# Two-layer trunk on one core: the order of two ScalarE copies, and a separate signal for the choice of experts

## What is computed

```python
x = layer_norm(ALPHA * x + h, ln1_g[i], ln1_b[i])
s  = sigmoid(x @ router_w)                  # 256 tokens x 64 experts
sb = s + router_bias                        # top 4 of 8 groups, then the top 8 experts of those
sel   = take_along_axis(s, eidx)
gates = sel / sum(sel) * 2.5
routed[tok] += gate * ((silu(x w1[e]) * (x w3[e])) w2[e])
shared = (silu(x sw1) * (x sw3)) sw2        # one expert that all tokens use
```

## Time and profile before

| what | value |
|---|---|
| median of three runs | 1353.06 us (1351.78 to 1354.09) |
| span of the profiled execution, first to last instruction | 1355.0 us |
| PE busy | 1308.7 us, 97% |
| DVE, ACT, POOL busy | 475.9, 310.8, 80.9 us |
| the 16 DMA engines | 83.1% of the span in the hardware queue; 462 MB |

### The profile page before, as it was taken

One profiled execution on the slowest core, in us unless ns is written; L12 is line 12 of the kernel. 1 busy time (PEld: TensorE's weight loads), 2 busy tenths in 40 slices (PEclk: granted clock), 3 DMA queues, 4 the chain that ended last, 5 costly groups with the idle time before them and its releaser, 6 DMA issues.

```text
span 1355.0 us, 23118 instructions
## 1 busy us (share of the span) xinstructions
PE 1308.7 (97%) x9746; PEld 751.7 (55%) x9746; DVE 475.9 (35%) x795; ACT 310.8 (23%) x746; POOL 80.9 (6%) x93
## 2 busy tenths in 40 slices
PE   9999999999999999998999999999999998999998
PEld 4555665555555455554498467655555554554543
DVE  1584533233332223324501146232333322233244
ACT  1244422121212211121210224222222221112112
POOL 2443100000000000000100021000000000000000
PEclk9999999999999999999999999999999999999999
DMA  9820679999999999999754427899999999999991
GB/s 305 303 96 32 252 304 415 421 421 420 421 420 421 421 422 420 420 421 383 245 188 163 189 82 275 308 418 421 421 421 421 420 421 421 421 421 421 420 360 69
DMA packets 83007, 462.01 MB, mean 341 GB/s; under 512 B 7008, under 2 KB 7232, under 8 KB 34528
## 3 DMA queue, kind: packets, MB, share of 16 engines
q1 hardware_dynamic: 80896, 454.16, 83.1%
q0 software_dynamic: 2016, 6.43, 1.6%
HBM read 459.52 MB, written 1.05 MB: 340 GB/s over the span
## 4 chain that ended last, share of the span: by engine, by line
PE 75%; DMA 19%; DVE 3%; issue 1%; ACT 1%; SPq 0%; DVEq 0%
PE ps L1227 26%; DMA ring<-in_exp_w_dram 19%; PE ps L1267 12%; PE ps L884 4%; PE ps L1413 4%; PE ps L1289 4%; PE ps L1166 4%; PE ps L1063 3%; PE ps L988 3%; PE ps L1135 2%; PE ps L1087 2%; PE ps L1237 1%; PE ps L1048 1%; PE ps L1127 1%; PE ps L904 1%
## 5 line engine op out<-in xcount | busy, mean ns | idle before, releaser
L1267 PE MATMUL ps<-ring,qkT 128*32 128x512 f32 x1984 | 232.9, 595 | 4.4 <-issue 3.1
L2120 DVE TENSOR_TENSOR o_tok<-ps,o_tok 128x1024 f32<-128x1024 f32 x124 | 150.7, 1223 | 157.4 <-PE ps L1289 157.4
L2125 DVE TENSOR_TENSOR y_lo<-ps,y_hi 128x1024 fp32r<-128x1024 f32 x62 | 75.9, 1225 | 214.1 <-ACT y_hi L1645 214.1
L1227 PE MATMUL ps<-ring,xT 128*64 128x256 f32 x1008 | 124.5, 385 | 14.7 <-DMA ring<-in_exp_w_dram 14.7
L1267 PEld LDWEIGHTS ps<-ring,qkT 128*32 128x32 f32 x1984 | 61.5, 109 | 129.3 <-issue 127.5
L1227 PE MATMUL ps<-ring,pT 128*64 128x256 f32 x992 | 124.3, 385 | 6.4 <-DMA ring<-in_exp_w_dram 6.4
L1620 ACT ACTIVATE roped<-ps 128x256 f32<-128x256 f32 x64 | 24.6, 385 | 455.7 <-PE ps L1227 455.7
L1227 PE MATMUL ps<-ring,proj 128*64 128x256 f32 x1008 | 121.8, 379 | 0.2 <-DMA ring<-in_exp_w_dram 0.2
L1227 PE MATMUL ps<-ring,gb_row 128*64 128x256 f32 x992 | 121.5, 379 | 0.0
L2109 DVE SCALAR_TENSOR_TENSOR roped<-roped,rows,ps 128x256 f32<-128x256 f32 x64 | 30.7, 480 | 236.9 <-ACT roped L1620 236.9
L1227 PEld LDWEIGHTS ps<-ring,xT 128*64 128x64 f32 x1008 | 71.0, 136 | 73.5 <-issue 36.1
(11 more groups left out here) (301 smaller groups left out, 1477.8 us busy)
## 6 DMA issues: line engine op xcount, KB each, us to landing
ring<-in_exp_w_dram SPq DMA_DIRECT2D x158, 2048.0 KB, 23.1
ring<-in_exp_w_dram SPq DMA_DIRECT2D x54, 1024.0 KB, 9.0
ring<-in_od_w_in_dram SPq DMA_DIRECT2D x6, 2048.0 KB, 8.8
ring<-in_ple_w_gate_dram SPq DMA_DIRECT2D x4, 2048.0 KB, 16.1
ring<-in_ev_w_in_dram SPq DMA_DIRECT2D x3, 2048.0 KB, 20.2
ring<-in_ev_w_o_dram SPq DMA_DIRECT2D x2, 2048.0 KB, 9.9
x_tok<-in_exp_w_dram SPq DMA_DIRECT2D x4, 1024.0 KB, 8.8
ring<-in_exp_w_dram SPq DMA_DIRECT2D x8, 512.0 KB, 16.5
```

Source lines behind the costliest of these rows:

```text
L1227: ins = pe.matmul(ps[b * SLOTS:(b + 1) * SLOTS, 2, w * FE:(w + 1) * FE], xe(odd, c)[:, u * P + b * SLOTS:u * P + (b + 1) * SLOTS], views[b ...
L1267: ins = pe.matmul(ps[q:q + TILE_SLOTS, 4 + half, :], hT[:, f, h0:h0 + TILE_SLOTS], down_rows(b, f, half), start=(f == 0), stop=(f == 1))
L2120: dve.tensor_tensor(ys, ps[:, bank:bank + 2, :], ys, ALU.add).then_inc(sem("y_added"), 1)
L2125: dve.tensor_tensor(y_lo[:, :], ps[:, 4:6, :].rearrange("p b n -> p (b n)"), y_hi[:, :], ALU.subtract)\
```

## The change

ACT copies a tile's transposes ahead of writing its rounded half, for both tiles and in both layers. In `choose`, the instruction that writes `chosen` now counts up a semaphore of its own, and PE waits for that one ahead of the place matmuls, where it waited for the finished gates.

```diff
 # ACT, both layers
                 rsqrt_guess()
+                copy_T("xT_act", tp, 0)
                 x_high(0)
-                copy_T("xT_act", tp, 0)
                 router_exp(0)
                 y_begin(0)
                 rsqrt_guess()
+                copy_T("xT_act", tp, 1)
                 x_high(1)
-                copy_T("xT_act", tp, 1)
                 router_exp(1)
 # DVE, choose
-                seq(dve.tensor_scalar(own, sb_, TAKEN, None, ALU.is_equal))
+                dve.tensor_scalar(own, sb_, TAKEN, None, ALU.is_equal).then_inc(sem("chosen"), 1)
+                dve.wait_ge(sem("chosen"), NT * L + t + 1)
                 seq(dve.tensor_tensor(g1, s, own, ALU.mult))
 # PE, ahead of the place matmuls
-                pe.wait_ge(sem("router_dve"), NT * (L + 1))
+                pe.wait_ge(sem("chosen"), NT * (L + 1))
```

The rest of the diff renames semaphores. Six that PE counts up once each in the compressed branch of layer 0 (`cmp_tp`, `cmp_h`, `cmp_kv`, `cmp_rep`, `cmp_sc`, `cmp_pT`, in that order) become one, `cmp_pe`, with the waits at 1 to 6; three that ACT counts up in layer 1 (`fox_abs`, `fox_e`, `fox_ln`) become `fox_act` with the waits at 1 to 3. One pair of lines of each:

```diff
-                    dve.wait_ge(sem("cmp_kv"), 1)
+                    dve.wait_ge(sem("cmp_pe"), 3)
-                    dve.wait_ge(sem("fox_ln"), 1)
+                    dve.wait_ge(sem("fox_act"), 3)
```

More of the change, by code:

```diff
@@ L641, in _ @@
                 if src == QA:
-                    pool.wait_ge(sem("cmp_h"), 1)
+                    pool.wait_ge(sem("cmp_pe"), 2)
                 for t in range(1 if src == QA else NT):
@@ L776, in attention @@
                             ins = pe.transpose(ps[:, 6, tt * P:(tt + 1) * P], cmp_s[:, tt, :], ident)
-                        ins.then_inc(sem("cmp_pT"), 1)
+                        ins.then_inc(sem("cmp_pe"), 1)
                     if 3 <= u < U + 3:
@@ L860, in compressed_scores @@
                                         small[:, 448:448 + 2 * CMP_PAD], start=True, stop=True)
-                ins.then_inc(sem("cmp_sc"), 1)
+                ins.then_inc(sem("cmp_pe"), 1)
             def transpose_queries(t):
@@ L946, in compressed_inputs @@
                         pe.transpose(ps[:, 5, 0:CMP_LEN], qkT[0:CMP_LEN, 16, 0:P], ident[0:CMP_LEN, 0:CMP_LEN])\
-                            .then_inc(sem("cmp_tp"), 1)
+                            .then_inc(sem("cmp_pe"), 1)
                     def compressed_hidden(part):
@@ L958, in compressed_hidden @@
                         if part == 3:
-                            ins.then_inc(sem("cmp_h"), 1)
+                            ins.then_inc(sem("cmp_pe"), 1)
                     def compressed_kv():
@@ L967, in compressed_kv @@
                                             small[0:HD, half * HD:(half + 1) * HD], start=True, stop=True)
-                        ins.then_inc(sem("cmp_kv"), 1)
+                        ins.then_inc(sem("cmp_pe"), 1)
                     def compressed_spread():
@@ L974, in compressed_spread @@
                         pe.matmul(ps[:, 4, 0:HD], const[0:CMP_PAD, C_REP:C_REP + P], small[0:CMP_PAD, 384:448],
-                                  start=True, stop=True).then_inc(sem("cmp_rep"), 1)
+                                  start=True, stop=True).then_inc(sem("cmp_pe"), 1)
                     def project_tile(j, t, between=()):
@@ L1459, in attention @@
                     if L == 0 and u == 4:
-                        act.wait_ge(sem("cmp_pT"), 1)
+                        act.wait_ge(sem("cmp_pe"), 6)
                         act.activation(small_pT, ps[:, 6, 0:SEQ], ACT.Copy).then_inc(sem("cmp_pT_copied"), 1)
@@ L1540, in _ @@
                     duplicate("roped", 3, 28)
-                    act.wait_ge(sem("cmp_h"), 1)
+                    act.wait_ge(sem("cmp_pe"), 2)
                     act.activation(small[0:HD, 160:160 + N_CMP], ps[0:HD, 4, 0:N_CMP], ACT.Exp, scale=-1.0)
@@ L1553, in _ @@
                     act.wait_ge(sem("fox_z"), 1)
[L1554 to L1558, removed]
+                    act.activation(fox_t, fox_zb, ACT.Abs).then_inc(sem("fox_act"), 1)
+                    act.wait_ge(sem("fox_act"), 1)
+                    act.activation(fox_t, fox_t, ACT.Exp, scale=-1.0).then_inc(sem("fox_act"), 1)
+                    act.wait_ge(sem("fox_act"), 2)
+                    act.activation(fox_t, fox_t, ACT.Ln, bias=1.0).then_inc(sem("fox_act"), 1)
                     for j in range(4):
@@ L1775, in compressed_max @@
             def compressed_max():
-                dve.wait_ge(sem("cmp_sc"), 1)
+                dve.wait_ge(sem("cmp_pe"), 5)
                 for t in range(NT):
@@ L1942, in compressed_blocks @@
                     def compressed_blocks():
-                        dve.wait_ge(sem("cmp_tp"), 1)
+                        dve.wait_ge(sem("cmp_pe"), 1)
                         seq(dve.tensor_copy(kvT, ps[:, 4, 0:SEQ]))
@@ L1987, in _ @@
                     topk_round(8)
-                    dve.wait_ge(sem("cmp_rep"), 1)
+                    dve.wait_ge(sem("cmp_pe"), 4)
                     dve.tensor_copy(small[0:HD, 448:448 + CMP_PAD], ps[0:HD, 5, 0:CMP_PAD])
@@ L2015, in _ @@
                        .then_inc(sem("fox_z"), 1)
-                    dve.wait_ge(sem("fox_abs"), 1)
+                    dve.wait_ge(sem("fox_act"), 1)
                     seq(dve.tensor_scalar(z, z, 0.0, None, ALU.min))
-                    dve.wait_ge(sem("fox_ln"), 1)
+                    dve.wait_ge(sem("fox_act"), 3)
                     dve.tensor_tensor(logf.rearrange("p t n -> p (t n)"), z, fox_t, ALU.subtract).then_inc(sem("logf"), 1)
```

## The result

The kernel takes **1357.11 us** (median of 8 runs, 1355.74 to 1359.55) against 1353.33 us for the kernel before (8 runs, 1351.78 to 1354.53). The ratio is 1.0028, with an interval of 1.0019 to 1.0037: **3.8 us slower, 2.6 to 5.0**.

The account below looks back on a forecast made before the run. PE was taken to bound the stage from first norm to experts, the weight stream the expert loop's end. A 1.8 us later gather in each of two layers gives 3.6 us: 1353.06 + 3.6 = 1356.7 us, range 1353.2 to 1358.4.

Parts of the forecast that it names:

- The copies: ACT's copies of tile 0 run first: second copy ends at 148.23 instead of 148.39, router gains at most 0.16 us.
- ACT's chain: Tile 0 on ACT: x_high and table load fall behind the copies; exponential starts at 151.56 instead of 150.54, 1.02 us late.
- The disputed price: ACT's table load: 1.28 us by the rows, about 2.66 us by the skill page, which would make the sum about 4.4 us.
- x_lo and the hold: Tile 0: POOL's x_lo, 150.32 to 153.21, holds the choice's first TENSOR_SCALAR on DVE until 153.26, 2.16 us late.
- the bounds: Delay of tile 0's first TENSOR_SCALAR: 1.02 us if POOL doesn't hold it, 2.16 us if it does; the upper was taken.
- the other bound: Rival: POOL doesn't hold the choice up; PE loses under 0.1 us a layer, 1353.2 us. Chance 0.13.
- PE: PE's transposes of tile 1 move from 162.05 to 163.28, 1.23 us; PE stands still for 1.4 us ahead of them.
- Tile 1 and the gather: Tile 1's TENSOR_SCALAR ends 2.76 us late, DVE has 0.58 us to spare; the gather starts 1.8 us late.
- The signal: `chosen`'s own signal to PE: worth nothing by itself; in the new order saves about 0.6 us at the gather.
- The rest of the layer: Everything after the stage, DMA-bound expert loop included, moves by PE's delay, since the weight stream starts afresh in each layer.
- The rival that the weight stream takes the stall up: PE loses 1.8 us in the stage and as much less later in the layer, up to 1353.1 us. Chance 0.07.
- The sum: 1.8 us a layer, two layers: 3.6 us, added to the median of 1353.06 us.

Follow-up runs that it names:

- e3: The changed kernel, with PE waiting for the finished gates again and the choice's scores kept in PSUM: 1353.55 us, ratio 0.9993 to the kernel before.
- e4: The kernel before, old ACT order and semaphores, with POOL computing x_lo twice over: 1360.06 us, ratio 1.0042 to the kernel before.
- e2: The changed kernel with ACT's old order, keeping the choice's own signal and the renamed semaphores: 1353.80 us, ratio 0.9996 to the kernel before.
- e1: The changed kernel with PE's place matmuls waiting for the finished gates again, copies still first: 1358.96 us, ratio 1.0035 to the kernel before.
- e7: The changed kernel with POOL's x_lo subtraction cut into four instructions of a quarter each: 1353.34 us, ratio 1.0003 to the kernel before.

## Why the prediction was right

Taken against the start of the tile-0 transposes (146.57 before, 146.69 after), step by step:

- **The copies.** Forecast to end at +1.66 us, against +1.82 before; they end at 147.93 + 0.49 = 148.42, which is +1.73. The router gains 0.1 us where at most 0.16 was forecast, and loses it at the next gap, as foreseen.
- **ACT's chain.** The exponential starts at +4.99, as forecast (151.56 - 146.57 = 4.99; now 151.68 - 146.69). The disputed price is settled by the rows: the table load takes 1.28 us and ends at 151.66, and the exponential starts 0.02 us later. The 2.66 us that the Trainium skill gives for a switch (ScalarE: Activation LUTs, What ACT_TABLE_LOAD costs) do not show here. The prediction's estimate by that page was loose by a little: with 1.38 us more the exponential would have started at 151.56 + 1.38 = 152.94, ahead of x_lo's end at 153.21, and only the TENSOR_SCALAR, due 0.36 us behind the exponential's start, would have come after it.
- **x_lo and the hold.** x_lo from +3.75 to +6.64 was forecast, +3.75 to +6.62 came; the TENSOR_SCALAR was forecast to end 0.05 us behind it and did. The choice between the bounds (1.02 us if not held, 2.16 us if held) was the one that decided: it ended 2.14 us late, and e3 and e4 show the hold to be the cause. The price that the prediction gave the other bound, under 0.1 us a layer, is about what e3 measures, 0.11 and 0.09. The rule of the Trainium skill (SBUF — State Buffer, Who interferes with whom), by which such an instruction waits for the whole of POOL's, holds for 64 columns too: 1.33 us instead of 0.195.
- **PE.** Transposes of tile 1 at +16.71 forecast, +16.69 measured; the gap was forecast as 1.4 us. From the start of the last shared-expert block it is 163.38 - 160.19 = 3.19 us to the transposes, against 162.05 - 160.17 = 1.88 in the same timeline of before, so 1.31 us; the profile's own 1.14 us is shorter, since the ends of matmuls are modelled.
- **Tile 1 and the gather.** The TENSOR_SCALAR ends 170.15 - 146.69 = 23.46 us in (23.50 forecast), the gather is at 29.74 (29.83 forecast). 1.70 and 1.65 us a layer instead of 1.8: `sel` is late by 2.06 us (175.52 - 146.69 against 173.34 - 146.57) where the TENSOR_SCALAR is late by 2.72, so DVE had 0.66 us to spare, not the 0.58 us of its idle row. PE had another 0.36: the gather started 0.51 us after `sel` was done before (174.10 to 174.61) and starts 0.15 us after it now (176.28 to 176.43).
- **The signal.** Forecast worth nothing alone, and 0.6 us a layer at the gather in the new order. It measured 0.0 (e2), and 0.73 and 0.75 (e1 against after): sized too small by some 0.1 us.
- **The rest of the layer.** Forecast to move one for one with the stage. SP's first weight load that waits for PE's expert matmuls shows it, before and then after:

```profile
182.51 0.33 SPq L472 DMA_DIRECT2D ring<-in_exp_w_dram  x1
```

```profile
184.33 0.33 SPq L472 DMA_DIRECT2D ring<-in_exp_w_dram  x1
```

From the transposes of tile 0 that is 35.94 us before and 37.64 after, 1.70 later, the same as the gather: the stream starts afresh later by all of the stall. Over the seven experiments and the change the difference by the ratio agrees with the stage within its interval: 3.35 us and 3.8, 4.83 and 4.7, 6.1 and 5.7. The rival that the weight stream takes the stall up would have left them near nothing.

The sum was 3.6 us; the stages show 3.35, the times 3.8 with 2.6 to 5.0. That the forecast of 1356.7 us lies within 0.4 us of the median is closer than that interval can tell, and so in part luck; what bears the mechanism out is the stage. The one weak step was to set the sum against the profiled span: the forecast of 1358.6 us for the profiled execution was missed by 4.5 us, since that span varies by more than the change. Carrying the sum over to the median of the runs kept this out of the predicted time.

## What to carry to other kernels

When work on one engine is moved, look up what it releases on the others, and lay that next to the clock of every chain that runs there: here two copies put first, for 0.1 us at the router, moved a POOL instruction of 2.9 us into the start of DVE's chain. A POOL elementwise instruction on SBUF beside a latency-bound DVE chain is safe only where the chain's TENSOR_SCALAR and two-input instructions don't come due; chain operands in PSUM took the hold away here, and short POOL instructions cut it to what is left of one of them. And judge a change of a few microseconds by the length of its stage in both traces, not by two spans.

## What the hardware showed that was not expected

- The hold is by instruction, and DVE gets in between two of POOL's: 0.20 us between two x_lo in e4, and at most 0.23 us beside four quarters in e7.
- With its first operand and its result in PSUM the TENSOR_SCALAR is not held (0.23 us beside x_lo in e3), nor is a TENSOR_TENSOR with one operand in PSUM and one in SBUF (0.23 us); with both in SBUF it took 2.23 us in e4.
- RECIPROCAL on SBUF is not held: 0.55 us beside the second x_lo of tile 1 in e4, as with POOL at rest in after.
- POOL itself is not slowed: x_lo takes 2.87 us with a held instruction waiting (after) and 2.88 us without (e3). Where the TENSOR_SCALAR got in first, in tile 1 of e4, it took 2.91.
